# Split products in another order: rounded x rounded, low weights x rounded input, rounded weights x low input

## The chip, the core and the metric

The kernel runs on one core of a Trainium2 chip (trn2). The metric is the time of one execution on the device in microseconds (us); the median of several runs is given. Matmuls run on TensorE (PE in the profile, its weight loads PEld), the other engines are VectorE (DVE), ScalarE (ACT), GpSimd (POOL) and SyncE (SP), which issues most of the DMAs here.

## What is computed

Two transformer-like blocks in float32 on 256 tokens (and 16 meta tokens in the first), width 2048. Cut to the products with large weight matrices, which is what the change touches:

```python
# first block, 272 rows
u = rms_norm(h, a_norm) @ a_w_in            # 2048 x 8192, gated recurrence per head
h = h + (o * silu(z)) @ a_w_out             # 2048 x 2048
kv = rms_norm(h, kv_norm) @ kv_w            # 2048 x 4112
# from here 256 rows
u = rms_norm(h, b_norm) @ b_w_in            # 2048 x 4096, attention with forgetting
h = h + (o * silu(z)) @ b_w_out             # 2048 x 2048
# second block
proj = rms_norm(x, norm1) @ w_in + b_in     # convolution and sliding-window attention
x = x + mixed @ w_out                       # 2048 x 2048
q = rms_norm(x, norm2) @ peer_w_q           # 2048 x 2048, then top 16 of 128 x 128 experts, 8 heads
hidden = gelu(xn @ u[expert]) * gate        # u, v: 16384 x 2048
y = sum over experts of hidden * v[expert]
```

The last two lines are computed densely: every expert's hidden value for every token, with a gate that is zero where the expert wasn't chosen.

## The kernel before

**Tiles.** Every large weight matrix is cut into tiles of 128 partitions x 2048 float32 (1 MB). A tile holds 16 blocks of 128 x 128, one for each step kk of the contraction (or, in the last stage, for each output block). 475 such tiles come through one ring of four buffers, `raw[:, q, :]`, loaded by DMAs on the SyncE queue, each of which waits on the semaphore `halves_done`, by which TensorE counts the half tiles that it has used up.

**The split.** A float32 weight is written as a sum of two numbers of the type fp32r. ScalarE makes the rounded part `whi` (`split_hi`, L422 to L428, half a tile at a time, four half-tile slots), VectorE or GpSimd the rest `wlo` = raw - whi in place of the raw tile (`split_lo`, L430 to L435); `w_lo_done[half]` counts those. The input has been split the same way earlier into `x[0]` (rounded) and `x[1]` (rest). The product is then the sum of three matmuls in one PSUM bank, (hi, x_hi), (hi, x_lo) and (lo, x_hi); (lo, x_lo) is left out.

**The five places with such a triple.** `project` (L437 to L453) makes one tile of a projection in 16 steps: it waits for `evacuated` (the bank is free), then for each half of the tile for `w_lo_done`, and then issues 8 steps of three matmuls; the last instruction of a half increments `halves_done`. It serves the recurrence's input product, the key/value product (both 272 columns) and the later ones with 256 columns, the output products among them. `out_piece` (L489 to L508) and `wout_piece` (L1424 to L1440) issue the first two tiles of an output product in pieces, as parts of its input become ready. `up_project` (L2025 to L2036) is the same as `project` for the tiles of u, called by `up_tensor` in two stages (segments 0 and 1). `down_tensor` (L2222 to L2246) takes a tile of v: here the 16 blocks go to 16 different half banks, the input is one expert's coefficient for 256 tokens (`e.coef_hi`, `e.coef_lo`, two buffers each), the same for all 16 steps, and the sums stay in all eight banks over 64 tiles. Its two stages run the same loop body on the same buffers; they are called the first and the second down stage below.

**Order.** Each engine runs its instructions in the order of the program. The stages follow each other as in the reference; between the triples of some stages stand small matmuls of the recurrence and of attention (float32 without split) and, in the up stages, of the gates (`spread_step`, bfloat16). The first input product of the second block (L464) works on unsplit float32 and has no triple. The triple's first line is L450, L502, L1436, L2033 or L2238; the next two lines are its second and third product.

Of the kernel before, what the change touches and what calls it, by code (L numbers as in the profile page):

```python
# [18 lines left out]
KT = D // P  # L19
META = 16  # L20
SEQ = 256
# [193 lines left out]
def build(nc, hT_in, params_in, consts_in, masks_in, pos_in, keys_in, w_in, u_in, v_in, out):  # L215
    with ExitStack() as ctx:
# [11 lines left out]
        e = Named()  # L228
# [208 lines left out]
        def project(te, t, x, cols, skipped=0, ps=None, halves=(0, 1)):  # L437
# [4 lines left out]
            for half in halves:  # L442
# [4 lines left out]
                for k in range(8):  # L447
                    kk = half * 8 + k
                    hi, lo = whi[:, slot, k * P:(k + 1) * P], wlo[:, t.q, kk * P:(kk + 1) * P]
                    te.matmul(ps, hi, x[0][:, kk, cols], start=(kk == 0), stop=False)  # L450
                    te.matmul(ps, hi, x[1][:, kk, cols], start=False, stop=False)  # L451
                    last = te.matmul(ps, lo, x[0][:, kk, cols], start=False, stop=(kk == KT - 1))  # L452
                last.then_inc(halves_done, 1)  # L453
# [35 lines left out]
        def out_piece(te, base, tile, kks):  # L489
# [6 lines left out]
            for kk in kks:  # L496
# [5 lines left out]
                te.matmul(ps, hi, x[0][:, kk, 0:n], start=(kk == 0), stop=False)  # L502
                te.matmul(ps, hi, x[1][:, kk, 0:n], start=False, stop=False)
                last = te.matmul(ps, lo, x[0][:, kk, 0:n], start=False, stop=(kk == KT - 1))
                if kk == 7 and tile == 0:
# [918 lines left out]
        def wout_piece(te, tile, k0):  # L1424
# [8 lines left out]
            for kk in (k0, k0 + 1):  # L1433
                slot, k = (2 * t.q + kk // 8) % 4, kk % 8
                hi, lo = whi[:, slot, k * P:(k + 1) * P], wlo[:, t.q, kk * P:(kk + 1) * P]
                te.matmul(ps, hi, xa[0][:, kk, 0:SEQ], start=(kk == 8), stop=False)  # L1436
                te.matmul(ps, hi, xa[1][:, kk, 0:SEQ], start=False, stop=False)
                last = te.matmul(ps, lo, xa[0][:, kk, 0:SEQ], start=False, stop=(kk == KT - 1))
            if k0 == KT - 2:
# [585 lines left out]
        def up_project(te, t, ps):  # L2025

            for half in range(2):
                te.wait_ge(w_lo_done[half], t.k + 1)
                slot = (2 * t.q + half) % 4
                for k in range(8):  # L2030
                    kk = half * 8 + k
                    hi, lo = whi[:, slot, k * P:(k + 1) * P], wlo[:, t.q, kk * P:(kk + 1) * P]
                    te.matmul(ps, hi, xb[0][:, kk, 0:SEQ], start=(kk == 0), stop=False)  # L2033
                    te.matmul(ps, hi, xb[1][:, kk, 0:SEQ], start=False, stop=False)  # L2034
                    last = te.matmul(ps, lo, xb[0][:, kk, 0:SEQ], start=False, stop=(kk == KT - 1))  # L2035
                last.then_inc(halves_done, 1)  # L2036
# [185 lines left out]
        def down_tensor(te, ch, g_):  # L2222
            te.wait_ge(evacuated, T_V[g_] - g_ * SEG)

            def body(i):
                for s in range(4):
# [4 lines left out]
                    for half in range(2):  # L2231
                        te.wait_ge(w_lo_done[half], t.k + 1)
                        slot = (2 * t.q + half) % 4
                        for k in range(8):
# [3 lines left out]
                            te.matmul(ps, hi, e.coef_hi[:, s % 2, :], start=(begins and kk % 2 == 0), stop=False)  # L2238
                            te.matmul(ps, hi, e.coef_lo[:, s % 2, :], start=False, stop=False)  # L2239
                            last = te.matmul(ps, lo, e.coef_hi[:, s % 2, :], start=False,   # L2240
                                             stop=(final and kk % 2 == 1))
# [261 lines left out]
```

## Time and profile before

| | us |
|---|---|
| median of 3 runs | 3110.28 (3110.05 to 3112.72) |
| profiled execution | 3118.69 |
| its span, first to last instruction | 3116.9 |
| TensorE busy, matmuls | 3042.5 (98%) |
| TensorE busy, weight loads | 2963.2 (95%) |
| VectorE busy | 1881.5 (60%) |
| ScalarE busy | 1633.1 (52%) |
| GpSimd busy | 664.7 (21%) |

A row of a group in the profile names the line, engine and operation, the tiles written and read, the shapes and how often (x), then busy time and the mean of one in ns, then the idle time of the engine ahead of it and what ended most of it. "128*128 128x272" is a weight block of 128 x 128 with an input of 128 partitions x 272 columns. Matmuls are pipelined: their records overlap, and a busy share of 98% says that TensorE always had a matmul under way, not that it was at its peak. The mean granted clock of TensorE over the span is 0.991 of full speed (2.4 GHz).

By stage: up to about 805 us 272 columns (recurrence, its output product, keys and values), then 256 columns: query and gate projection with attention to about 1065 us, its output product to about 1150, convolution and sliding-window attention to about 1400, the third output product and the expert queries (with the first u tiles) to about 1790, first up stage to 1999, first down stage to 2363, second up stage to 2752, second down stage to the end.

### The profile page before, as it was taken

The page shows a single profiled execution, that of the slowest core. Times are in us where ns is not written, and L with a number is a line of the kernel's source. Part 1 is how long each engine was busy: PE and PEld are TensorE (multiplying, and loading weights), DVE is VectorE, ACT ScalarE, POOL GpSimd, SP SyncE. Part 2 cuts the span into 40 slices and gives each one's busy share as a digit, 9 for nine tenths or more (in the row PEclk, how much of TensorE's full clock was granted, in tenths as well). Part 3 has the DMA queues.
Part 4 walks back from the last instruction along what each step waited for, and adds up shares of the span by engine and source line. Part 5 has one row for each costly group of instructions (what it writes and reads, how often), then busy time and mean ns, then how long its engine had stood idle before and what let it go on. Part 6 is the DMA issues. An engine that isn't in the chain of part 4 may idle for free.

```text
span 3116.9 us, 63458 instructions
## 1 busy us (share of the span) xinstructions
PE 3042.5 (98%) x25252; PEld 2963.2 (95%) x25252; DVE 1881.5 (60%) x3274; ACT 1633.1 (52%) x2607; POOL 664.7 (21%) x292
## 2 busy tenths in 40 slices
PE   8999999999999999979999999999999999999999
PEld 7999998999999998869999989999999999999999
DVE  5555555645544558757677788644447865554445
ACT  5766765566787643565444443444444444444443
POOL 3333332444444333114444400000000000000000
PEclk9999999999999999999999999999999999999999
DMA  5443443444444454315555544555554455555554
GB/s 197 140 147 136 147 142 116 169 169 166 168 139 137 147 181 139 133 55 178 175 187 178 187 136 138 177 186 188 179 185 165 158 180 189 185 178 188 187 188 165
DMA packets 72288, 506.67 MB, mean 163 GB/s; under 512 B 7904, under 2 KB 10464, under 8 KB 11232
## 3 DMA queue, kind: packets, MB, share of 16 engines
q1 hardware_dynamic: 71584, 503.16, 47.2%
q8 instruction: 91, 1.49, 0.2%
q10 hardware_dynamic: 576, 1.72, 0.2%
q14 instruction: 37, 0.30, 0.0%
HBM read 502.75 MB, written 2.10 MB: 162 GB/s over the span
## 4 chain that ended last, share of the span: by engine, by line
PE 92%; DVE 5%; ACT 2%; issue 1%; DMA 0%; SPq 0%; DVEq 0%; ACTq 0%
PE bank L450 12%; PE bank L451 12%; PE bank L452 12%; PE bank L464 5%; PE bank L2238 4%; PE bank L2240 4%; PE banks L2238 4%; PE banks L2240 4%; PE bank L2239 4%; PE banks L2239 4%; PE banks L2033 3%; PE banks L2034 3%; PE banks L2035 3%; PE bank L2033 2%; PE bank L2034 2%; PE bank L2035 2%
## 5 line engine op out<-in xcount | busy, mean ns | idle before, releaser
L427 ACT ACTIVATE whi<-raw 128x1024 fp32r<-128x1024 f32 x898 | 941.4, 1057 | 988.8 <-PE bank L452 394.5
L434 DVE TENSOR_TENSOR wlo<-raw,whi 128x1024 fp32r<-128x1024 f32 x667 | 815.5, 1234 | 462.7 <-ACT whi L427 461.5
L434 POOL TENSOR_TENSOR wlo<-raw,whi 128x1024 fp32r<-128x1024 f32 x231 | 607.9, 2632 | 982.9 <-ACT whi L427 982.8
L450 PE MATMUL bank<-xa_hi,whi 128*128 128x272 f32 (+1 forms) x2000 | 583.5, 292 | 5.9 <-DVE wlo L434 4.6
L451 PE MATMUL bank<-xa_lo,whi 128*128 128x272 f32 (+1 forms) x2000 | 573.6, 287 | 0.0
L452 PE MATMUL bank<-xa_hi,wlo 128*128 128x272 f32 (+1 forms) x2000 | 572.6, 286 | 0.0
L450 PEld LDWEIGHTS bank<-xa_hi,whi 128*128 128x128 f32 x2000 | 377.3, 189 | 11.1 <-issue 6.0
L451 PEld LDWEIGHTS bank<-xa_lo,whi 128*128 128x128 f32 x2000 | 378.5, 189 | 1.3
L452 PEld LDWEIGHTS bank<-xa_hi,wlo 128*128 128x128 f32 x2000 | 377.5, 189 | 0.0
L450 PE MATMUL bank<-xb_hi,whi 128*128 128x256 f32 (+1 forms) x1120 | 318.5, 284 | 0.5 <-DVE wlo L434 0.5
L451 PE MATMUL bank<-xb_lo,whi 128*128 128x256 f32 (+1 forms) x1120 | 316.5, 283 | 0.0
L452 PE MATMUL bank<-xb_hi,wlo 128*128 128x256 f32 (+1 forms) x1120 | 315.9, 282 | 0.0
L2238 PE MATMUL bank<-e_coef_hi,whi 128*128 128x256 f32 x1024 | 288.8, 282 | 4.8 <-issue 4.8
L2238 PE MATMUL banks<-e_coef_hi,whi 128*128 128x256 f32 x1024 | 287.9, 281 | 0.0
L2239 PE MATMUL bank<-e_coef_lo,whi 128*128 128x256 f32 x1024 | 286.8, 280 | 0.0
L2240 PE MATMUL bank<-e_coef_hi,wlo 128*128 128x256 f32 x1024 | 286.5, 280 | 0.0
L2239 PE MATMUL banks<-e_coef_lo,whi 128*128 128x256 f32 x1024 | 286.1, 279 | 0.0
L2240 PE MATMUL banks<-e_coef_hi,wlo 128*128 128x256 f32 x1024 | 286.0, 279 | 0.0
L2033 PE MATMUL banks<-xb_hi,whi 128*128 128x256 f32 x768 | 216.8, 282 | 1.7 <-DVE hT L2297 1.2
L2034 PE MATMUL banks<-xb_lo,whi 128*128 128x256 f32 x768 | 216.3, 282 | 0.0
L2035 PE MATMUL banks<-xb_hi,wlo 128*128 128x256 f32 x768 | 215.9, 281 | 0.0
L2034 PE MATMUL bank<-xb_lo,whi 128*128 128x256 f32 x768 | 215.3, 280 | 0.0
(434 smaller groups left out, 6734.7 us busy)
## 6 DMA issues: line engine op xcount, KB each, us to landing
raw<-in_w SPq DMA_DIRECT2D x251, 1024.0 KB, 4.8
raw<-in_v SPq DMA_DIRECT2D x128, 1024.0 KB, 5.2
raw<-in_u SPq DMA_DIRECT2D x96, 1024.0 KB, 4.9
hT<-in_hT SPq DMA_DIRECT2D x4, 544.0 KB, 7.8
out<-hT SPq DMA_DIRECT2D x8, 256.0 KB, 2.4
r_keys<-in_keys ACTq DMA_DIRECT2D x1, 1024.0 KB, 5.2
c_mask<-in_masks ACTq DMA_DIRECT2D x1, 320.0 KB, 3.0
g_mask<-in_masks SPq DMA_DIRECT2D x1, 272.0 KB, 11.7
```

Source lines behind the costliest of these rows:

```text
L427: act.activation(whi[:, (2 * t.q + half) % 4, :], raw[:, t.q, half * 1024:(half + 1) * 1024], ACT.Copy).then_inc(w_hi_done, 1)
L434: eng.tensor_tensor(wlo[:, t.q, at], raw[:, t.q, at], whi[:, slot, :].bitcast(F32), ALU.subtract).then_inc(w_lo_done[half], 1)
L450: te.matmul(ps, hi, x[0][:, kk, cols], start=(kk == 0), stop=False)
L451: te.matmul(ps, hi, x[1][:, kk, cols], start=False, stop=False)
L452: last = te.matmul(ps, lo, x[0][:, kk, cols], start=False, stop=(kk == KT - 1))
L464: last = te.matmul(ps, raw[:, t.q, kk * P:(kk + 1) * P], x[:, kk, 0:n], start=(kk == 0), stop=(kk == KT - 1))
L2033: te.matmul(ps, hi, xb[0][:, kk, 0:SEQ], start=(kk == 0), stop=False)
L2034: te.matmul(ps, hi, xb[1][:, kk, 0:SEQ], start=False, stop=False)
L2035: last = te.matmul(ps, lo, xb[0][:, kk, 0:SEQ], start=False, stop=(kk == KT - 1))
L2238: te.matmul(ps, hi, e.coef_hi[:, s % 2, :], start=(begins and kk % 2 == 0), stop=False)
L2239: te.matmul(ps, hi, e.coef_lo[:, s % 2, :], start=False, stop=False)
L2240: last = te.matmul(ps, lo, e.coef_hi[:, s % 2, :], start=False, stop=(final and kk % 2 == 1))
```

## The change

In all five places the second and the third product of a triple change places: after (hi, x_hi) comes (lo, x_hi), and (hi, x_lo) is last. The flags `start` and `stop` and the increments stay at the first and the last instruction of their groups. Waits, buffers and counts are the same.

```diff
--- before.py
+++ after.py
@@ -448,8 +448,9 @@
                     kk = half * 8 + k
                     hi, lo = whi[:, slot, k * P:(k + 1) * P], wlo[:, t.q, kk * P:(kk + 1) * P]
                     te.matmul(ps, hi, x[0][:, kk, cols], start=(kk == 0), stop=False)
-                    te.matmul(ps, hi, x[1][:, kk, cols], start=False, stop=False)
-                    last = te.matmul(ps, lo, x[0][:, kk, cols], start=False, stop=(kk == KT - 1))
+                    te.matmul(ps, lo, x[0][:, kk, cols], start=False, stop=False)
+                    last = te.matmul(ps, hi, x[1][:, kk, cols], start=False,
+                                     stop=(kk == KT - 1))
                 last.then_inc(halves_done, 1)
 
         RESUMED = (T_WOUT, T_WOUT + 1)
@@ -500,8 +501,9 @@
                 slot, k = (2 * t.q + kk // 8) % 4, kk % 8
                 hi, lo = whi[:, slot, k * P:(k + 1) * P], wlo[:, t.q, kk * P:(kk + 1) * P]
                 te.matmul(ps, hi, x[0][:, kk, 0:n], start=(kk == 0), stop=False)
-                te.matmul(ps, hi, x[1][:, kk, 0:n], start=False, stop=False)
-                last = te.matmul(ps, lo, x[0][:, kk, 0:n], start=False, stop=(kk == KT - 1))
+                te.matmul(ps, lo, x[0][:, kk, 0:n], start=False, stop=False)
+                last = te.matmul(ps, hi, x[1][:, kk, 0:n], start=False,
+                                 stop=(kk == KT - 1))
                 if kk == 7 and tile == 0:
                     last.then_inc(halves_done, 1)
                 if kk == KT - 1:
@@ -1434,8 +1436,9 @@
                 slot, k = (2 * t.q + kk // 8) % 4, kk % 8
                 hi, lo = whi[:, slot, k * P:(k + 1) * P], wlo[:, t.q, kk * P:(kk + 1) * P]
                 te.matmul(ps, hi, xa[0][:, kk, 0:SEQ], start=(kk == 8), stop=False)
-                te.matmul(ps, hi, xa[1][:, kk, 0:SEQ], start=False, stop=False)
-                last = te.matmul(ps, lo, xa[0][:, kk, 0:SEQ], start=False, stop=(kk == KT - 1))
+                te.matmul(ps, lo, xa[0][:, kk, 0:SEQ], start=False, stop=False)
+                last = te.matmul(ps, hi, xa[1][:, kk, 0:SEQ], start=False,
+                                 stop=(kk == KT - 1))
             if k0 == KT - 2:
                 last.then_inc(halves_done, 2)
 
@@ -2031,8 +2034,9 @@
                     kk = half * 8 + k
                     hi, lo = whi[:, slot, k * P:(k + 1) * P], wlo[:, t.q, kk * P:(kk + 1) * P]
                     te.matmul(ps, hi, xb[0][:, kk, 0:SEQ], start=(kk == 0), stop=False)
-                    te.matmul(ps, hi, xb[1][:, kk, 0:SEQ], start=False, stop=False)
-                    last = te.matmul(ps, lo, xb[0][:, kk, 0:SEQ], start=False, stop=(kk == KT - 1))
+                    te.matmul(ps, lo, xb[0][:, kk, 0:SEQ], start=False, stop=False)
+                    last = te.matmul(ps, hi, xb[1][:, kk, 0:SEQ], start=False,
+                                     stop=(kk == KT - 1))
                 last.then_inc(halves_done, 1)
 
         def up_tensor(te, ch, g_):
@@ -2236,8 +2240,8 @@
                             ps = bank[kk // 2][:, kk % 2 * SEQ:(kk % 2 + 1) * SEQ]
                             hi, lo = whi[:, slot, k * P:(k + 1) * P], wlo[:, t.q, kk * P:(kk + 1) * P]
                             te.matmul(ps, hi, e.coef_hi[:, s % 2, :], start=(begins and kk % 2 == 0), stop=False)
-                            te.matmul(ps, hi, e.coef_lo[:, s % 2, :], start=False, stop=False)
-                            last = te.matmul(ps, lo, e.coef_hi[:, s % 2, :], start=False, 
+                            te.matmul(ps, lo, e.coef_hi[:, s % 2, :], start=False, stop=False)
+                            last = te.matmul(ps, hi, e.coef_lo[:, s % 2, :], start=False,
                                              stop=(final and kk % 2 == 1))
                             if final and g_ == SEGS - 1 and kk % 2 == 1:
                                 last.then_inc(bank_final, 1)
```

## Rows read from the trace of the kernel before

**Rows 1.** The page's parts 1, 2 and 4: busy time, 40 slices, chain.

```profile
PE 3042.5 (98%) x25252; PEld 2963.2 (95%) x25252; DVE 1881.5 (60%) x3274; ACT 1633.1 (52%) x2607; POOL 664.7 (21%) x292
...
PE   8999999999999999979999999999999999999999
PEld 7999998999999998869999989999999999999999
...
PEclk9999999999999999999999999999999999999999
DMA  5443443444444454315555544555554455555554
...
PE 92%; DVE 5%; ACT 2%; issue 1%; DMA 0%; SPq 0%; DVEq 0%; ACTq 0%
```

**Rows 2.** The page's part 5, the groups that cut a weight tile in two.

```profile
L427 ACT ACTIVATE whi<-raw 128x1024 fp32r<-128x1024 f32 x898 | 941.4, 1057 | 988.8 <-PE bank L452 394.5
L434 DVE TENSOR_TENSOR wlo<-raw,whi 128x1024 fp32r<-128x1024 f32 x667 | 815.5, 1234 | 462.7 <-ACT whi L427 461.5
L434 POOL TENSOR_TENSOR wlo<-raw,whi 128x1024 fp32r<-128x1024 f32 x231 | 607.9, 2632 | 982.9 <-ACT whi L427 982.8
```

**Rows 3.** Groups by line and form on TensorE: first products of triples; busy us, mean ns.

```profile
L450 PE MATMUL bank<-xa_hi,whi 128*128 128x272 f32 x1552 | 458.3, 295 | 3.0 <-DVE wlo L434 1.7 <-DVE xa_lo L833 1.2
...
L2238 PE MATMUL bank<-e_coef_hi,whi 128*128 128x256 f32 x1024 | 288.8, 282 | 4.8 <-issue 4.8
...
L450 PE MATMUL bank<-xb_hi,whi 128*128 128x256 f32 x896 | 253.0, 282 | 0.0
L2033 PE MATMUL banks<-xb_hi,whi 128*128 128x256 f32 x768 | 216.8, 282 | 1.7 <-DVE hT L2297 1.2 <-DVE e_hid L2157 0.5
...
L450 PE MATMUL bank<-xa_hi,whi 128*128 128x256 f32 x448 | 125.2, 279 | 3.0 <-DVE wlo L434 3.0
...
L450 PE MATMUL banks<-xb_hi,whi 128*128 128x256 f32 x384 | 108.0, 281 | 0.0
...
L450 PE MATMUL bank<-xb_hi,whi 128*128 128x272 f32 x224 | 65.4, 292 | 0.5 <-DVE wlo L434 0.5
...
L1436 PE MATMUL bank<-xa_hi,whi 128*128 128x256 f32 x32 | 11.2, 349 | 2.3 <-DVE xa_lo L1624 2.3
L502 PE MATMUL bank<-xb_hi,whi 128*128 128x272 f32 x32 | 11.0, 344 | 3.0 <-DVE xb_lo L904 3.0
```

**Rows 4.** Windows of 100 us: TensorE busy (matmuls), granted clock, DMA share.

```profile
2010.00:2110.00 100.00, 100.00 (x846) 1.00 0.53 184
...
2860.00:2960.00 100.00, 100.00 (x863) 1.00 0.55 186
...
2630.00:2730.00 100.00, 100.00 (x855) 1.00 0.55 187
1530.00:1630.00 100.00, 100.00 (x856) 1.00 0.55 186
```

**Rows 5.** Timeline of TensorE, 272 columns: start, length; first and last row.

```profile
697.84 0.29 PE L450 MATMUL bank<-xa_hi,whi 128*128 128x272 f32 x1
...
707.23 0.29 PE L450 MATMUL bank<-xa_hi,whi 128*128 128x272 f32 x1
```

**Rows 6.** The page's part 5: the weight loads of one triple.

```profile
L450 PEld LDWEIGHTS bank<-xa_hi,whi 128*128 128x128 f32 x2000 | 377.3, 189 | 11.1 <-issue 6.0
L451 PEld LDWEIGHTS bank<-xa_lo,whi 128*128 128x128 f32 x2000 | 378.5, 189 | 1.3
L452 PEld LDWEIGHTS bank<-xa_hi,wlo 128*128 128x128 f32 x2000 | 377.5, 189 | 0.0
```

**Rows 7.** Timeline of TensorE's weight loads (PEld) in the up stage: start, length.

```profile
2600.15 0.19 PEld L2034 LDWEIGHTS bank<-xb_lo,whi 128*128 128x128 f32 x1
2600.26 0.19 PEld L2035 LDWEIGHTS bank<-xb_hi,wlo 128*128 128x128 f32 x1
```

**Rows 8.** Timeline of TensorE's matmuls in the up stage: first two and last.

```profile
2600.14 0.28 PE L2033 MATMUL bank<-xb_hi,whi 128*128 128x256 f32 x1
2600.26 0.28 PE L2034 MATMUL bank<-xb_lo,whi 128*128 128x256 f32 x1
...
2618.78 0.27 PE L2033 MATMUL banks<-xb_hi,whi 128*128 128x256 f32 x1
```

**Rows 9.** Waits of TensorE: what it waited for, us in total, times, longest.

```profile
PE bank L450 <- DVE wlo L434: 5.1, 4, 1.8
...
PE bank L450 <- DVE xa_lo L833: 1.2, 1, 1.2
```

**Rows 10.** Timeline of both down stages: first and last start of a stretch.

```profile
2100.30 0.28 PE L2238 MATMUL banks<-e_coef_hi,whi 128*128 128x256 f32 x1
...
2118.79 0.28 PE L2238 MATMUL banks<-e_coef_hi,whi 128*128 128x256 f32 x1
...
2900.20 0.28 PE L2238 MATMUL banks<-e_coef_hi,whi 128*128 128x256 f32 x1
...
2918.70 0.28 PE L2238 MATMUL bank<-e_coef_hi,whi 128*128 128x256 f32 x1
```

## Prediction

> **What bounds the kernel now.** I read the page first. TensorE is busy 98% of the span with 25252 matmuls, VectorE 60%, ScalarE 52%, the DMA engines about half, and TensorE also makes 92% of the chain that ended last; its granted clock is near full throughout [rows 1]. The reader should take two things from this. The end is set by one engine, and nothing else is close behind it: the machinery that cuts each weight tile in two halves (L427 and L434) has hundreds of microseconds in which it waits, much of that for TensorE itself [rows 2]. So a time added to or taken from each matmul reaches the end nearly one for one, in both directions.
>
> Second, I counted what the change touches. In the groups by line and form, the first of the three products of a step stands at L450 (1552 + 224 with 272 columns; 896 + 384 + 448 with 256), L2033 (2 x 768), L2238 (2 x 1024), L502 (32 + 32) and L1436 (32) [rows 3] (of L2033, L2238 and L502 one of two rows alike stands). That makes 1776 + 32 = 1808 triples of 272 columns and 1728 + 1536 + 2048 + 64 = 5376 of 256, together 7184 triples or 21552 matmuls, 85% of all.
>
> Third, what one of these matmuls costs. Busy time is no price here: a matmul is recorded at about 0.28 us while the next starts 0.12 us after it, so records overlap. The price is the pitch from start to start. In a window in which nothing else runs it is (window + 0.28 us) / count, since matmuls that begin just before the window are counted too. The first down stage gives 100.28/846 = 118.5 ns, the second down stage 100.28/863 = 116.2 ns, the up stage and the third output projection 100.28/855 to 856 = 117.2 ns [rows 4]. With 272 columns 25 triples take 707.23 - 697.84 = 9.39 us, or 125.2 ns a matmul [rows 5]. A stream of columns at 2.4 GHz would need 106.7 and 113.3 ns, so 10 to 12 ns of each pitch are something else. That remainder is what an order of products could move.
>
> **The change, part by part.** It removes no instruction and adds none. Before, a step kk issues (hi, x_hi), (hi, x_lo), (lo, x_hi); after, (hi, x_hi), (lo, x_hi), (hi, x_lo). Four things have to be costed.
>
> *Weight loads.* Before, the same block hi is the stationary operand twice in a row; afterwards no two neighbours share one. Had the second load been left out before, the change would add one load to each triple. The page shows it isn't left out: L451 has its own 2000 loads, at 189 ns like L450 and L452 [rows 6]. And each load starts as the matmul before it starts (load of L2034 at 2600.15, matmul of L2033 at 2600.14) [rows 7, 8], three loads to three matmuls before and after. Cost in number: 0.
>
> *Waits.* In `project`, `up_project` and `down_tensor` TensorE waits for the low weights of a half (w_lo_done) ahead of the first product, not ahead of the product that reads them, and for both halves of the input by one semaphore. So no product that is moved earlier starts to wait, and none that is moved later is freed. In the whole span TensorE waits only 5.1 us ahead of L450 for low weights, four times [rows 9]; that wait stands where it stood. Cost: 0, and no gain either.
>
> *Releases.* The increments of halves_done and bank_final hang on the third instruction of a triple in both versions. The weight slots, PSUM banks and the queue of weight loads on the SyncE queue are released by an instruction with the same number. The queues of SyncE, ScalarE, VectorE and GpSimd get not one instruction more or in another place. Cost: 0 beyond what TensorE's own pace does. The opening product with start=True stays first and the closing one with stop=True stays last, so accumulation in the bank is framed the same.
>
> *The pitch itself.* This is the only term that can be other than zero, and the trace of before doesn't have the new order. What it has are bounds. The pitch isn't a constant of the shape: the two down stages run the same instructions on the same buffers, without idle time of TensorE between tiles, and differ by 118.5 - 116.2 = 2.3 ns a matmul, each steadily for hundreds of microseconds [rows 4]. Nor is it the same for the three places in a triple. Means over 53 triples of the up stage give 115.7, 118.1 and 117.9 ns for first to second, second to third and third to the next first [rows 8]; over 52 triples of the first down stage 119.2, 117.7, 118.7; over 53 of the second 116.8, 117.7, 114.5 [rows 10]; and with 272 columns 126.4, 124.0, 125.2 [rows 5]. No place is always the cheap one: the pair that shares its weights is cheapest in the up stage, dearest in the first down stage and with 272 columns. I read this as a pipeline that settles into one of several rhythms, depending on how it was started and on what is read side by side, and not as a price of an operand pair.
>
> So the bounds are: all 256-column matmuls at the best pitch seen, and all at the worst. Up stage and projections are 3328 triples = 9984 matmuls, the first down stage 3072, the second 3072. Best: 9984 x (117.2 - 116.2) + 3072 x 2.3 = 10.0 + 7.1 = 17 us less. If the 5424 matmuls of 272 columns also came to the best remainder seen (116.2 + 16 columns at 2.4 GHz, 6.7 ns, = 122.9; 2.3 ns less), another 12 us: 29 us less in all. Worst: 9984 x 1.3 + 3072 x 2.3 = 13.0 + 7.1 = 20 us more. The value I take is 0, since the nearest row is the present average of the same instructions and no row says to which side a new rhythm would lie.
>
> The Trainium skill (TensorE: Matmul & The Clock Gate, section "Step-by-step: what each phase is for") says that the engine reads the streamed operand and the weights by two independent ports, so that loading the next weights takes nothing from the running matmul. By that rule the order can't matter at all: the result would be that of the forecast, with no chance on either side. The same page (section "Back-to-back issue gap") gives N/2.4 + 2.5 ns, 109.2 for 256 columns, as the gap of isolated matmuls; the trace has 116.2 to 118.5 [rows 4]. Something between neighbours costs time here that this rule doesn't name, and this is why I don't lean on it.
>
> **Sum.** The profiled execution took 3118.69 us, of which 3116.9 are the span. The known terms add 0, so its counterpart after is 3118.7. The median of the runs shown is 3110.28, or 8.4 less than the profiled one; 3118.7 - 8.4 = 3110.3 us. About 0.2% (6.2 us) is what a measurement of this kernel can tell from no change. That is 0.29 ns on each of the 21552 matmuls, a quarter of one percent of the pitch, and the two down stages already differ by eight times that. This is why "same" is likeliest but not nearly certain.
>
> **Rivals.**
>
> *A better rhythm (faster).* With nothing changed but the rhythm of the first down stage, from 118.5 to the 116.2 of the second, the kernel gains 3072 x 2.3 = 7.1 us: 3103 us. For it: the stage runs the same instructions as its faster twin, so a shorter rhythm exists for them, and the 272-column stages have the largest remainder too (125.2 - 113.3 = 11.9 ns). Against it: nothing in the change aims at it. Chance of faster by over 0.2%: 0.31, reaching to 3093 where the projections join in.
>
> *The pair that shares its weights was cheap (slower).* In the up stage the pitch behind the first product is 2.3 ns under the other two [rows 8], and there the next load is of the block already loaded. If that is why, the new order loses it wherever the up stage's rhythm rules, in 3328 triples: 3328 x 2.3 = 7.7 us, 3118 us. Its point of decision is that a price below 1.9 ns (6.2/3328) would not show. Extended to all 7184 triples it would be 16.5 us, 3127. Against it: in the first down stage and with 272 columns the same pair is the dearest of the three. Chance, with the second down stage falling to its twin's 118.5 (also + 7.1 us, 3117): 0.27.
>
> *It doesn't do what it says.* If consecutive uses of one weight block had been merged before, the number of loads would rise by 7184 and the time by far more than any bound above. The equal counts [rows 6] rule it out: under 0.01. A wait that becomes late is likewise excluded by where the waits stand.
>
> **How the numbers follow.** Same within 0.2%: 0.42, with 3110.3 as the time and 3104 to 3116.5 as its own range. Faster 0.31, slower 0.27. For 8 in 10 the range takes in the down stage's rhythm on both sides (3103, 3117), the shared pair at its price, and part of what the projections and the 272-column stages could add: 3097 to 3124. The ends 3081 and 3130 of the bounds need every stage to go the same way and are left out.
>
> **What would show it.** After: again 25252 matmuls and as many loads, and the waits of TensorE unchanged. Then the windows of the down, up and projection stages: 846, 863 and 855 matmuls in 100 us if the pitch stood still. If the first down stage has 863, the faster rival holds; if the up stage falls to about 850 or the second down stage to 846, the slower one. The prediction is wrong if the new order forces a rhythm of its own outside 116.2 to 118.5 ns, or if a stage settles differently in every run of the same kernel. The clock is no part of the argument; should a stretch be granted 1.2 GHz that had 2.4 before, that difference is to be set aside first.

## The result: 1.0% slower

The changed kernel takes 3147.59 us (median of 4 runs, 3141.90 to 3148.75), the kernel before 3111.50 beside it; the ratio is 1.0102 (95% interval 1.0089 to 1.0114). The profiled execution took 3147.00 us with a span of 3145.2, against 3118.69 and 3116.9 before: 28.3 us more. The forecast was 3110.3 in a range of 3097 to 3124. The loss is in TensorE's pace alone, as the next lines show.

The page of the changed kernel first: busy time of each engine with the number of instructions, then the shares of the chain that ended last. Below it what TensorE waited for in front of L450 (us in total, times, longest).

```profile
PE 3074.5 (98%) x25252; PEld 2994.7 (95%) x25252; DVE 1882.6 (60%) x3274; ACT 1633.7 (52%) x2607; POOL 664.2 (21%) x292
...
PE 91%; DVE 6%; ACT 2%; issue 1%; DMA 0%; SPq 0%; DVEq 0%; ACTq 0%
```

```profile
PE bank L450 <- DVE wlo L434: 5.1, 4, 1.8
```

The same 25252 matmuls and 25252 loads [rows 1], TensorE busy for 32.0 us more, VectorE and ScalarE to within 1.1 us of before, and the wait for low weights 5.1 us in 4 pieces as in [rows 9]. So no wait was added and no work; each matmul keeps TensorE longer. The windows show where (TensorE busy, matmuls in brackets, granted clock, DMA share, GB/s), and one stretch with 272 columns, the first row and the row 23 triples (69 matmuls) later:

```profile
1530.00:1630.00 100.00, 100.00 (x834) 1.00 0.52 176
2210.00:2310.00 100.00, 100.00 (x846) 1.00 0.55 188
...
2630.00:2730.00 100.00, 100.00 (x832) 1.00 0.53 178
...
2960.00:3060.00 100.00, 100.00 (x851) 1.00 0.54 184
```

```profile
693.47 0.29 PE L450 MATMUL bank<-xa_hi,whi 128*128 128x272 f32 x1
...
702.13 0.29 PE L450 MATMUL bank<-xa_hi,whi 128*128 128x272 f32 x1
```

The third output projection has 834 matmuls where it had 856, the second up stage 832 where it had 855: 100.28/832 = 120.5 ns instead of 117.3 [rows 4]. The first down stage stands where it stood, at 846 or 118.5 ns; the second has 851, 117.8 ns instead of 116.2. With 272 columns it is (702.13 - 693.47)/69 = 125.5 ns, 0.3 more than in [rows 5]. Cut at the starts of the first up stage, first down stage and second up stage and at the last step of the latter (1776.5, 2000.7, 2366.2 and 2751.4 us before; 1788.1, 2013.8, 2380.7 and 2775.1 after) the 28.3 us fall into 11.6 ahead of the first up stage, 1.5 in it, 1.4 in the first down stage, 9.2 in the second up stage and 4.6 in the second down stage.

The timeline of TensorE in the second up stage has the form of the loss (start, length). The first line is the last product of a tile; the tile of the next lines begins at 2642.43 with step 0.

```profile
2642.30 0.30 PE L2038 MATMUL banks<-xb_lo,whi 128*128 128x256 f32 x1
2642.43 0.28 PE L2036 MATMUL bank<-xb_hi,whi 128*128 128x256 f32 x1
...
2643.50 0.28 PE L2036 MATMUL bank<-xb_hi,whi 128*128 128x256 f32 x1
2643.62 0.29 PE L2037 MATMUL bank<-xb_hi,wlo 128*128 128x256 f32 x1
2643.74 0.30 PE L2038 MATMUL bank<-xb_lo,whi 128*128 128x256 f32 x1
2643.88 0.28 PE L2036 MATMUL bank<-xb_hi,whi 128*128 128x256 f32 x1
```

In step 3 the first two pitches are 0.12 us (starts 2643.50, 2643.62 and 2643.74), and the third product is followed only after 0.14. Averaged over some 30 tiles from 2540 to 2740 us, by place and step, the pitches in ns are:

| step kk | before: hi x_hi, hi x_lo, lo x_hi | after: hi x_hi, lo x_hi, hi x_lo |
|---|---|---|
| 0, 4, 8, 12 | 116.7, 118.3, 116.7 | 120.0, 116.7, 117.5 |
| 1, 5, 9, 13 | 116.7, 117.5, 120.0 | 119.2, 118.3, 117.5 |
| 2, 6, 10, 14 | 112.5, 116.7, 117.5 | 124.2, 115.8, 120.0 |
| 3, 7, 11, 15 | 114.2, 120.8, 119.2 | 116.7, 127.5, 133.3 |

In both kernels this is the same to 0.1 ns in steps kk, kk + 4, kk + 8 and kk + 12 of every tile, whatever bank, weight slot or DMA goes with it. It is a rhythm of twelve matmuls, and in the changed kernel it has two long ones, 127.5 and 133.3. Four steps are also the distance at which the input comes back to the same place in a line of 256 bytes: one step lies 272 x 4 = 1088 bytes behind the other, and 4 x 1088 = 17 x 256, while 1088 and 2 x 1088 are no multiples. That made the two theories for the experiments. **A, pairing:** a weight block loaded twice in a row is cheap, and the change lost that. **B, placement:** what counts is where in such a line the input begins and which weight block is loaded beside it; the order changes who meets whom. (The length 256 is read off the period: of the powers of two, it is the one that divides 4 x 1088 but not 2 x 1088.)

### The profile page after: what moved, and what is told of

Read it like the earlier page. It is cut to its first block, busy times and chain, and to the rows that moved or that the text cites. A ratio compares the mean times of both kernels' runs of the same rounds, so it can differ in the third digit from the quotient of the medians.

```text
span 3145.2 us, 63458 instructions
## 1 busy us (share of the span) xinstructions
PE 3074.5 (98%) x25252; PEld 2994.7 (95%) x25252; DVE 1882.6 (60%) x3274; ACT 1633.7 (52%) x2607; POOL 664.2 (21%) x292
## 4 chain that ended last, share of the span: by engine, by line
PE 91%; DVE 6%; ACT 2%; issue 1%; DMA 0%; SPq 0%; DVEq 0%; ACTq 0%
PE bank L450 12%; PE bank L452 12%; PE bank L451 12%; PE bank L2242 4%; PE bank L2243 4%; PE bank L2244 4%; PE banks L2242 4%; PE banks L2243 4%; PE banks L2244 4%; PE bank L465 4%; PE banks L2036 3%; PE banks L2038 3%; PE bank L2038 3%; PE bank L2036 3%; PE banks L2037 3%; PE bank L2037 3%
## 5 line engine op out<-in xcount | busy, mean ns | idle before, releaser
L450 PE MATMUL bank<-xa_hi,whi 128*128 128x272 f32 (+1 forms) x2000 | 587.7, 294 | 4.8 <-DVE wlo L434 4.6
L450 PEld LDWEIGHTS bank<-xa_hi,whi 128*128 128x128 f32 x2000 | 378.8, 189 | 10.0 <-issue 6.0
L450 PE MATMUL bank<-xb_hi,whi 128*128 128x256 f32 (+1 forms) x1120 | 321.5, 287 | 0.5 <-DVE wlo L434 0.5
L2036 PE MATMUL bank<-xb_hi,whi 128*128 128x256 f32 x768 | 218.5, 284 | 0.0
```

## Experiments

In all runs below "up pitch" is the pitch in the second up stage without other work in it (2530 to 2730 us), read from windows as above, and "down" the two down stages. Times are medians, ratios are to the kernel before on the same chip.

### Which places carry the loss

The new order in `down_tensor` alone, and everywhere but there. Edits: the diff of the change, cut to its last hunk, or without it.

> The new order in the down stages alone. Expected from the stage readings: no more than 7 us either way on each of the two, 3104 to 3122 us, and 117.2 ns in the projections and up stages. If the down stages carried the loss it would be 3130 or more.

> The new order everywhere but in the down stages. Expected: 9984 matmuls of 256 columns at 120.5 instead of 117.3 ns is 32 us, 5424 of 272 at 125.6 instead of 125.25 is 2 us; 3135 to 3150 us, that is the whole loss.

Measured: down alone 3118.36 us, 1.0026 (1.0015 to 1.0038), up pitch 117.2, down 117.8 and 118.5 ns. All but down: 3140.82 us, 1.0098 (1.0065 to 1.0131), up pitch 120.5, down 116.3 and 118.5. A window of the first down stage and one of the second up stage with the new order in the down stages alone:

```profile
2210.00:2310.00 100.00, 100.00 (x851) 1.00 0.53 183
...
2630.00:2730.00 100.00, 100.00 (x855) 1.00 0.55 186
```

Against the 3110.86 us of the kernel before on that chip, the projections and up stages carry 30.0 us and the down stages 7.5, together 37.5 for the 36.1 of the whole change. So most of the loss, but not all, is that of the projections and up stages. The 9984 matmuls x 3.2 ns would be 32 us, and it comes out lower where other small matmuls break into the rhythm (query projection 119.2 ns, first up stage 119.7). The 5424 matmuls of 272 columns add about 2 us (125.6 ns where it was 125.25).

### Two other orders

```diff
# low weights first
-te.matmul(ps, hi, x[0][:, kk, cols], start=(kk == 0), stop=False)
-te.matmul(ps, hi, x[1][:, kk, cols], start=False, stop=False)
-last = te.matmul(ps, lo, x[0][:, kk, cols], start=False, stop=(kk == KT - 1))
+te.matmul(ps, lo, x[0][:, kk, cols], start=(kk == 0), stop=False)
+te.matmul(ps, hi, x[0][:, kk, cols], start=False, stop=False)
+last = te.matmul(ps, hi, x[1][:, kk, cols], start=False, stop=(kk == KT - 1))
# low input first
+te.matmul(ps, hi, x[1][:, kk, cols], start=(kk == 0), stop=False)
+te.matmul(ps, hi, x[0][:, kk, cols], start=False, stop=False)
+last = te.matmul(ps, lo, x[0][:, kk, cols], start=False, stop=(kk == KT - 1))
```

> Order (lo, x_hi), (hi, x_hi), (hi, x_lo) in all five places: the two products with the same weight block are neighbours again, and the low weights come first. Theory A (pairing: loading a block that was just loaded is cheap, and the change lost that): time of before, 3111 us, 117.2 ns in the second up stage. Theory B (alignment: the pitch depends on where in a 256-byte line the input of a step begins, since 1088 bytes lie between two steps, and on which weight block is loaded beside it): another fixed rhythm of four steps; time not tied to 3111, anything from 3090 to 3160, with the same rhythm in all stages of 256 columns.

> Order (hi, x_lo), (hi, x_hi), (lo, x_hi): the neighbours with the same weight block stay, only the two inputs are exchanged. x_hi and x_lo lie a multiple of 256 bytes apart. Theory A: 3111 us. Theory B: in the projections and the up stages exactly the pitches of before (117.2 ns), by place in the triple and by step; the down stages alone may differ, by no more than 7 us each.

Low weights first: 3126.67 us, 1.0054 (1.0034 to 1.0073), up pitch 118.0 ns, with 272 columns 126.2 to 126.4. The pair with one weight block is back and the time of before is not: theory A gave 3111. Low input first: 3120.68 us, 1.0038 (1.0021 to 1.0054); the up pitch is 117.2 and equal to before in every place and step to 0.2 ns, and the difference in time comes from the down stages, 117.8 and 118.5 ns. This fits both theories in the up stage. In total it missed A's 3111, and B's allowance of 7 us for each down stage covers it.

### The input at the same place in every step

```diff
-te.matmul(ps, hi, x[0][:, kk, cols], ...)
+te.matmul(ps, hi, x[0][:, kk // 4 * 4, cols], ...)
```

and so for all inputs outside the down stages, once in the changed order and once in that of before.

> The order of the changed kernel, but every product outside the down stages reads the input block of step kk // 4 * 4 instead of kk, so that all inputs begin at the same place of a 256-byte line (this leaves three quarters of the input out of the products). Theory A: the pitch stays at 120.5 ns in the second up stage, time 3147 us. Theory B: the outliers of 127 and 133 ns in every fourth step are gone, the pitch falls to 116 to 118.5 ns, time 3105 to 3125 us.

> The order of the kernel before with the same reading of block kk // 4 * 4 (three quarters of the input left out). Theory A: 3111 us and still a few us to tens of us under the run with the changed order. Theory B: no period of four steps, and a pitch close to that of the changed order with aligned inputs, within 1.5 ns.

Changed order 3135.98 us, 1.0089 (1.0066 to 1.0112); order of before 3129.68 us, 1.0059 (1.0028 to 1.0090). The up pitch is 119.05 ns in both, window for window:

```profile
2530.00:2630.00 100.00, 100.00 (x843) 1.00 0.55 186
2630.00:2730.00 100.00, 100.00 (x843) 1.00 0.54 182
```

```profile
2530.00:2630.00 100.00, 100.00 (x843) 1.00 0.53 180
2630.00:2730.00 100.00, 100.00 (x843) 1.00 0.55 188
```

The upper fence is the changed order, the lower that of before. I had expected 116 to 118.5 ns, and the value came out above that: the size was missed. The kinds agree with B: no step stands out any more, and the order has lost its effect. By place it is (after) 118.7, 118.6, 119.9 and (before) 119.9, 118.8, 118.5. Read by what is loaded next (high for the rounded block, low for the rest), the two are one list to 0.1 ns: high after high costs 119.9, low after high 118.7 or 118.8, high after low 118.6 or 118.5. In the order of before the "high after high" is the repeated block, in the changed order it is the next step's block, and both cost the same. That ends theory A: a repeated block is not cheaper. The medians of the two still lie 6 us apart, with ranges that overlap; their profiles differ in the down stages, which this edit left alone (118.5 and 117.8 ns in the changed order, 116.3 and 118.5 in the other).

### Both kinds of weights placed alike

```diff
-        tensor(ctx, "gap", [P, P + 16])
+        tensor(ctx, "gap", [P, 232])
         token = tensor(ctx, "token", [P, 24])
         whi = tensor(ctx, "whi", [P, 4, D // 2], F32R)
+        tensor(ctx, "gap2", [P, 168])
         hT = tensor(ctx, "hT", [P, KT, L])
```

> The changed order; the array of rounded weights is moved by 352 bytes, so that the rounded and the low block of a step begin at the same place modulo 512 bytes (before: 96 bytes apart modulo 256), inputs stay where they were modulo 1024. Theory B (place of weights against place of input) says: with both kinds of weights placed alike, and both inputs placed alike, the machine can't tell the two orders apart. So the second up stage has the same pitch here and in the next run, within 0.1 ns, instead of 120.6 against 117.2. A theory in which the repeated block matters (A) expects the two to differ still by about 3 ns.

> The order of before with the same move of the rounded weights by 352 bytes. Theory B: same pitch as the run above in projections and up stages; which value it is, between 116 and 121 ns, the theory doesn't say. Theory A: 117.2 ns.

Changed order 3130.11 us, 1.0043 (1.0023 to 1.0063); order of before 3128.43 us, 1.0049 (1.0032 to 1.0066). Windows of both, the changed order above:

```profile
2530.00:2630.00 100.00, 100.00 (x843) 1.00 0.54 181
2630.00:2730.00 100.00, 100.00 (x843) 1.00 0.55 187
```

```profile
2530.00:2630.00 100.00, 100.00 (x844) 1.00 0.55 184
2630.00:2730.00 100.00, 100.00 (x844) 1.00 0.55 184
```

Both have 118.9 ns, and by place and step they agree to 0.1 ns in all twelve values (the longest is 125.0 in the second place of step 3 in both). The 3.3 ns that lay between the orders are gone once a high and a low block of a step begin at the same place of a line. Theory A asked for 3 ns between them.

### Inputs or weights moved by 64 bytes

```diff
 # inputs by 64 bytes
+        tensor(ctx, "gap2", [P, 16])      # ahead of hT
 # weights by 64 bytes, inputs by 256
+        tensor(ctx, "gap0", [P, 16])      # ahead of wlo
+        tensor(ctx, "gap2", [P, 48])      # ahead of hT
```

> The changed order; all arrays from the residual on, the inputs among them, are moved by 64 bytes, weights stay. If the outliers (127.5 and 133.3 ns, in steps 3, 7, 11 and 15) belong to an address of the input, they move to steps 2, 6, 10 and 14 and the mean pitch of the second up stage stays 120.56. If they belong to the number of the step or to the program, they stay in 3, 7, 11 and 15.

> The changed order; both arrays of weights are moved by 64 bytes and the inputs by 256. If the distance between weights and input decides, the outliers move to steps 0, 4, 8 and 12, pitch still 120.56 ns. If the place of the input alone decides, they stay in steps 3, 7, 11 and 15.

3143.30 us, 1.0090 (1.0057 to 1.0123), and 3149.37 us, 1.0109 (1.0077 to 1.0142). The changed kernel was also run once more as it is:

> The changed kernel once more. Expected: 120.6 ns in most stages of 256 columns, or its other rhythm of 118.9 in some of them, as the runs with moved arrays showed side by side; each stage that sits at 118.9 takes off 1.7 ns a matmul (5 us for the second up stage).

It gave 3143.37 us, 1.0101 (1.0069 to 1.0132), and as half expected its second up stage was this time in another rhythm, 118.9 ns with a single long matmul of 129. In the profiles of the two moved kernels the second up stage has that rhythm too, so the three can be laid side by side: a tile's beginning (the tile changes bank group there, "bank" to "banks" or back) and the long matmul. First the changed kernel as it is, then inputs moved, then weights moved:

```profile
2648.52 0.28 PE L2036 MATMUL banks<-xb_hi,whi 128*128 128x256 f32 x1
...
2649.58 0.29 PE L2036 MATMUL banks<-xb_hi,whi 128*128 128x256 f32 x1
2649.71 0.28 PE L2037 MATMUL banks<-xb_hi,wlo 128*128 128x256 f32 x1
```

```profile
2640.72 0.28 PE L2043 MATMUL bank<-xb_hi,whi 128*128 128x256 f32 x1
...
2641.43 0.29 PE L2043 MATMUL bank<-xb_hi,whi 128*128 128x256 f32 x1
2641.56 0.28 PE L2045 MATMUL bank<-xb_hi,wlo 128*128 128x256 f32 x1
```

```profile
2646.01 0.29 PE L2044 MATMUL bank<-xb_hi,whi 128*128 128x256 f32 x1
2646.14 0.28 PE L2046 MATMUL bank<-xb_hi,wlo 128*128 128x256 f32 x1
```

The 0.13 us stand 1.06 us after the start of the tile, 0.71 us, and 0: at the first product of step 3, of step 2 and of step 0. Moving the input forward by 64 bytes brings the place one step earlier, moving the weights forward by 64 bytes one step later. It is not the long matmul alone: all twelve values by place and step move along with it, to 0.2 ns. The distance between weights and input decides. The expectation named the rhythm with 127.5 and 133.3 for both; that one stands in the first up stage of the third kernel, at step 0 as foretold (120.6 ns in its last 45 us, with 127.3 and 133.3 in step 0 and the other ten values moved on by one step), but the mean of the second up stage, foretold as 120.56, was 118.9 in both.

### A scan of the low weights' place

In `up_project` the low block is read 32 x m bytes further on, m changing every 8 tiles of the second up stage (`j // 8` in the unrolled part, four loops of two turns behind it):

```diff
-hi, lo = whi[:, slot, k * P:(k + 1) * P], wlo[:, t.q, kk * P:(kk + 1) * P]
+at = kk * P + 8 * m - (64 if m and k == 7 else 0)
+hi, lo = whi[:, slot, k * P:(k + 1) * P], wlo[:, t.q, at:at + P]
```

> A scan inside one run, order of before. In the second up stage every 8 tiles read the low weights 32 x m bytes further on (m = 0 to 7; tiles 8m to 8m + 7), in the first up stage every 4 tiles, there with the rounded weights 32 bytes further on too. So the products read shifted weight blocks and are another computation; counts and shapes are unchanged. Theory B: each m has a pitch of its own between 116 and 121 ns, 117.2 at m = 0, and 118.9 at m = 5, where the low weights lie like the rounded ones modulo 256 bytes (as with both arrays moved level). Theory A, or any in which only order or program counts: 117.2 ns for all m.

> The same scan in the changed order. Theory B: 120.6 (or 118.9, its other rhythm) at m = 0, and at m = 5 the same 118.9 ns as the scan in the order of before, to 0.1 ns; at the other m the two orders may differ by up to 4 ns in either direction. If the changed order is slower at every m, then it is slower by itself and not by the placement; if at some m it is as fast or faster, the 3 ns belong to the placement.

One execution each, 3122.66 and 3135.02 us. Mean pitch of the last 96 matmuls of each stretch, without those that have a gate's matmul between them, in ns:

| m | 0 | 1 | 2 | 3 | 4 | 5 | 6 | 7 |
|---|---|---|---|---|---|---|---|---|
| order of before | 117.6 | 119.1 | 118.3 | 117.8 | 117.8 | 118.3 | 117.8 | 117.2 |
| changed order | 119.0 | 116.2 | 118.9 | 117.8 | 118.9 | 118.3 | 119.2 | 118.1 |

m = 0 to 2 have the gates' small matmuls between them and are less settled. At m = 5, where both kinds of weights lie alike, the orders agree, as B says, and not only in the mean: all twelve values by place and step are within 1 ns of each other (with the moved arrays it was 0.1).

At m = 3 the means agree too (117.8), but there the values differ by up to 5 ns (first two places of step 0: 117.5 and 117.5 before, 113.3 and 113.3 changed), so that equality is chance. At m = 4 in both orders, and at 6 and 7 in the changed one, the pattern comes back only after eight steps; the scan reads the block of every eighth step 256 bytes further back, which may be why.

The value at m = 5 is 118.3 and not the 118.9 foretold, and B didn't ask for 118.9: with the moved arrays the rounded weights had come to the place of the low ones, here the low ones go to the place of the rounded, 160 bytes on, which is no multiple of the 64 bytes by which the input moves from step to step.

Most of all, at m = 1 the order that costs 1% is the faster one, by 2.9 ns. The first up stages of the two runs moved the rounded weights too; their stretches are only 4 tiles long, mostly with gate matmuls in them, and I draw nothing from them.

### The decisive pair: 32 bytes of padding

```diff
+        tensor(ctx, "gap0", [P, 8])       # ahead of wlo
-        tensor(ctx, "gap", [P, P + 16])
+        tensor(ctx, "gap", [P, 136])
```

Only the low weights (and `raw`, which shares their place) move. In the scan nothing moved but the address from which TensorE reads the low weights; the DMAs and VectorE wrote where they always do. So the two tell apart whether the reading or the writing of that array matters.

> The changed order in full, with one placement altered: 32 bytes of padding ahead of the low weights and 32 less behind them, so that only they (and the raw tiles in the same place) move, as at m = 1 of the scan. Theory B: 116.2 ns in the up stages, where the changed order alone had 120.6 and the order of before 117.2. If projections of 256 columns follow, 9984 x 1.0 ns = 10 us less than before; stages of 272 columns and the down stages unknown, 5 us either way: 3095 to 3110 us, below both kernels. Theory A, or the order being slow by itself: 3140 to 3150 us.

> The order of before with the same 32 bytes. Theory B: 119.1 ns in the up stages, 9984 x 1.9 = 19 us more, 3125 to 3140 us, so that the same change of order, which costs 1% at the old place, gains about 1% here. Theory A: 3111 us.

| | changed order | order of before |
|---|---|---|
| as it was | 3147.59, ratio 1.0102 | 1 |
| low weights 32 bytes on | 3113.95, ratio 1.0015 (1.0004 to 1.0026) | 3147.55, ratio 1.0117 (1.0095 to 1.0140) |

Second up stage and second down stage of the two, the changed order above:

```profile
2630.00:2730.00 100.00, 100.00 (x864) 1.00 0.55 189
2860.00:2960.00 100.00, 100.00 (x852) 1.00 0.56 188
```

```profile
2630.00:2730.00 100.00, 100.00 (x839) 1.00 0.55 187
2860.00:2960.00 100.00, 100.00 (x836) 1.00 0.52 180
```

864 matmuls are 116.1 ns, the best up pitch of all runs; 839 are 119.5. By place and step both agree to 0.5 ns with m = 1 of the scan, where that has settled, in the last four steps of its tiles (the order of before has 124.2 and 130.8 in steps 1 and 2 here, 124.3 and 130.8 there), so it is TensorE's reading that counts and not where the DMAs and VectorE write. The same edit that costs 1.0% at the old place saves 1.1% here (3147.55 to 3113.95 us). The order isn't slow by itself.

The order of before came out slower than its 3125 to 3140: the forecast held the down stages still, and they ran at 120.0 ns in both halves, where the changed order has 117.8 at this place. They carry 13.6 of the 42.5 us between the two profiles.

Yet this version is not under the kernel before, where 3095 to 3110 was expected. Its up stages and projections are, by 1.1 ns, all but the second output projection (118.3 ns where it was 117.2); its down stages both stand at 117.8 ns, where those of before can both stand at 116.3. 6144 x 1.5 ns = 9 us are given back there, about what the 9312 others gain. The profiled executions agree with that (spans of 3110.8 us, and 3110.0 for the kernel before with both down stages at 116.3, in the next section); the medians on one chip are 5.1 us apart, which these terms don't explain.

### Does an unchanged program keep its pitch?

> The kernel before, once more, to see whether an unchanged program takes the same pitches twice. Expected: projections and up stages at 117.2 ns again; the down stages, whose inputs lie at the same address in every step, may sit at another of the values seen so far (116.3, 117.8, 118.5 ns) than in the first profile (118.5 and 116.3). If both come out as before, what sets them is in the program and not in how it was started.

3112.09 us, 1.0003 (0.9992 to 1.0014). Its windows in the first down stage and second up stage:

```profile
2110.00:2210.00 100.00, 100.00 (x862) 1.00 0.54 187
2630.00:2730.00 100.00, 100.00 (x856) 1.00 0.54 184
```

The up stage has its 856 again. The first down stage has 862, not the 846 of [rows 4]: 116.3 instead of 118.5 ns with the same program, and the span is 3110.0 us, 6.9 less than in the first profile, which is 3072 x 2.2 ns. So the down stages fall into one of several rhythms from one execution to the next. Three more profiles have the down code and the placement of before in their down stages (the input held in place and the scan, each in the order of before, and the new order everywhere but down): with this kernel's two that makes ten stages in the order of before, five at 116.3 ns, one at 117.8 and four at 118.5. That is likely a large part of the spread of 3105 to 3122 us that the kernel before showed; only profiled executions show the pitch, so it isn't measured for the others. The changed order at the same placement also has ten stages on record, four at 117.8 and six at 118.5, and none at 116.3. So here too the order matters, by which rhythms come: 0.9 ns between the two means, 5 us over 6144 matmuls, beside the 7.5 us measured.

The changed up stage does the same between 120.6 and 118.9. The chip is not what picks: on the chip that gave 118.9, the kernel with the new order everywhere but in the down stages, whose up stage is the same code, ran at 120.5. What picks, no run shows.

### Two attempts at a version that beats both

Both start from the version with 32 bytes and change the down stages: the first puts (lo, coef_hi) first in `down_tensor`, the second moves the coefficients.

```diff
 # first
+te.matmul(ps, lo, e.coef_hi[:, s % 2, :], start=(begins and kk % 2 == 0), stop=False)
+te.matmul(ps, hi, e.coef_hi[:, s % 2, :], start=False, stop=False)
+last = te.matmul(ps, hi, e.coef_lo[:, s % 2, :], start=False,
 # second
+            tensor(st, "gap_c", [P, 8])
             e.coef_hi = tensor(st, "e_coef_hi", [P, 2, SEQ], F32R)
```

> The changed order with the low weights 32 bytes further on (116.1 ns in the up stages), and in the down stages (lo, coef_hi), (hi, coef_hi), (hi, coef_lo), which at the old place ran at 116.3 ns in both. Down stages were 117.8 ns in the version without this. If the down stages come to 116.3: 6144 x 1.5 = 9 us less than the 3114 of that version, 3105 us, under the kernel before; if this order at the new place is one of the slow ones (120 ns), 3127 us.

> The changed order with the low weights 32 bytes further on, and the rounded coefficients of the down stages 32 bytes further on as well; nothing else differs. Only the down stages can move: 117.8 ns if their pitch doesn't depend on the place of their input, another of the values between 116.1 and 120 ns if it does; total 3104 to 3128 us, and the up stages stay at 116.1 ns.

3123.57 us, 1.0037 (1.0023 to 1.0052), down 120.0 ns in both halves (two of its ten executions took 3112 to 3113 us, with no profile to say in what rhythm); and 3123.07 us, 1.0045 (1.0028 to 1.0062), down 119.1 in both. The up pitch stayed at 116.1. The order that ran at 116.3 at the old place is among the slow ones here, and 32 bytes of the coefficients alone cost 1.3 ns. The effect holds in the down stages too, whose input stays in place; neither version beats the kernel before.

## Why the prediction was wrong

**What bounds the kernel: right.** TensorE's 32.0 us more of busy time came out as 28.3 us of span, with 3.7 us less idle time between; no other engine hid them.

**Weight loads, waits, releases: right.** Counts and waits are those of before. The repeated block was no saving, which the equal load counts said and the runs with the input held in place show in ns (119.9 for both kinds of "high after high").

**The pitch: wrong, and this is the step that failed.** "The value I take is 0", with bounds from "all 256-column matmuls at the best pitch seen, and all at the worst", 118.5 ns. The pitches seen in one order are no bounds for another: the changed order ran at 120.6, and the order of before at 119.5 with its weights 32 bytes on. The term for 9984 matmuls had + 13.0 us as its worst and would have needed 9984 x 3.3 = 33 us; everything but the down stages measured + 30.0 us (3140.82 against 3110.86). The term for the down stages was + 7.1 at its worst and measured + 7.5. The text saw that it could be so ("a rhythm of its own outside 116.2 to 118.5 ns") and left it out of the range.

**What I had in hand and didn't use.** "No place is always the cheap one" was read as a pipeline that settles in a rhythm by how it was started; that it also depends "on what is read side by side" stood there, but no term came of it. In the up stage it isn't chance: by step the trace of before already had a period of four (112.5 ns in the first place of every step 2, 6, 10, 14), and that period points to the 1088 bytes between steps. I averaged over steps and lost it. For the down stages the reading was right in part: the unchanged program took another pitch in the next profile, but which pitches come depends on the order too.

**The rivals.** The slower rival had the right sign and the wrong reason: the shared pair at 2.3 ns and 3118 us; the pair isn't cheap, and putting it back with the low weights first left 3127. Its price was also read low: over 35 tiles the up stage has 115.0, 118.3 and 118.3 ns by place, not the 115.7, 118.1 and 117.9 of the 53 triples, so that the rival's own sum would have been 3328 x 3.3 = 11 us, 3121. That this pair was the dearest in the first down stage and with 272 columns, the argument against that rival, holds (119.7 and 126.2 ns over the same stretches). The faster rival's rhythm (116.3 in the first down stage) did come, in the unchanged kernel.

**The Trainium skill's rule** (TensorE: Matmul & The Clock Gate, "Step-by-step: what each phase is for"), that loading the next weights takes nothing from the running matmul, isn't borne out at this level: moving the low weights by 32 bytes changed the up pitch from 120.6 to 116.1 ns in one order and from 117.2 to 119.5 in the other. Through which part of the machine weights and input get in each other's way no run shows; that it goes by their distance is shown, the mechanism is open.

## What to carry to other kernels

If TensorE bounds a kernel and its matmuls run at more than their columns' time, look at the byte placement of the weights against the inputs: here it was worth about 1% in either direction. An order of products can't be judged at one placement: try each order at a few paddings of 32 bytes, since the best order flips. Read pitch per place and per step, not as one mean, and look for the period at which operand addresses come back. Before a difference of a few us is put down to an edit, profile the unchanged kernel twice.

## What the runs showed of the hardware

- A stream of load and matmul pairs in fp32r with 256 columns had a pitch between 116.1 and 120.6 ns in the second up stage and the down stages, at a granted clock of 1.00 (106.7 would be the columns alone at 2.4 GHz), fixed for hundreds of microseconds and, in the up stage of the kernels before and after, the same to 0.1 ns at the same step of every tile.
- It follows the distance between the place of the weights and of the input: 64 bytes on the input move the long matmul one step earlier, 64 bytes on the weights one step later. With both kinds of weights alike (118.9 ns) or with the input held at one place (119.05 ns), the order of the products makes no difference to the up stage's pitch.
- The same program can take one of several pitches in one stage, from one execution to the next: 116.3 or 118.5 ns in the down stage of the kernel before, 118.9 or 120.6 in the up stage of the changed one. In the down stage that was worth 6.9 us of the span between two profiles of the same kernel.
- Two neighbouring matmuls with the same weight block still issue two weight loads (2000 of 2000 at 189 ns each, [rows 6]), and the second was no cheaper: with the input held in place, 119.9 ns whether the next block was the same or another of the same array.
